# Head norm of mixer B's prompt on 32 partitions by 128 columns, and ScalarE's third key copy ahead of the prompt's exponential

## What is computed

```
a = jax.nn.softmax(jnp.where(mask, s, -jnp.inf), axis=-1)
attn = a[:, :, 0] - lam * a[:, :, 1]
o = jnp.einsum('bhqk,bkhe->bqhe', attn, v)
def diff_head_norm(o, g, lam_init):
    o = o * lax.rsqrt(jnp.mean(o * o, -1, keepdims=True) + RMS_EPS) * g
    return o * (1.0 - lam_init)
```

## Time and profile before

| | us |
|---|---|
| median of 3 runs | 1525.13 |
| lowest and highest | 1523.01, 1525.96 |
| the profiled execution's own time | 1522.43 |
| its span, first to last instruction | 1520.6 |
| attention stage within it | about 660 to 1010 |
| last head norm and start of the output projection | about 1010 to 1031 |

### The profile page before, as it was taken

One profiled execution on the slowest core, in us unless ns is written; L12 is line 12 of the kernel. 1 busy time (PEld: TensorE's weight loads), 2 busy tenths in 40 slices (PEclk: granted clock), 3 DMA queues, 4 the chain that ended last, 5 costly groups with the idle time before them and its releaser, 6 DMA issues.

```text
span 1520.6 us, 31196 instructions
## 1 busy us (share of the span) xinstructions
PE 1429.7 (94%) x12051; PEld 1247.0 (82%) x12051; DVE 943.1 (62%) x1823; ACT 610.3 (40%) x1160; POOL 286.8 (19%) x300
## 2 busy tenths in 40 slices
PE   4999999999999999989999988889899999999996
PEld 4788899999998788856666655559799999999995
DVE  2222473699845743645666666666799943899554
ACT  4322541344413422245555555552554422454323
POOL 1000330455200200010010000000066501555000
PEclk8999999999999999999999999999999999999998
DMA  9996222333223133368999998853133223333221
GB/s 313 386 365 225 56 85 84 103 100 89 73 83 115 51 106 109 122 233 281 340 332 338 341 321 273 312 187 88 29 91 95 85 77 97 100 91 96 65 70 63
DMA packets 217583, 245.98 MB, mean 162 GB/s; under 512 B 10655, under 2 KB 154649, under 8 KB 217442
## 3 DMA queue, kind: packets, MB, share of 16 engines
q1 hardware_dynamic: 217218, 243.63, 48.6%
q10 hardware_dynamic: 224, 0.39, 0.1%
HBM read 236.91 MB, written 7.08 MB: 160 GB/s over the span
## 4 chain that ended last, share of the span: by engine, by line
PE 68%; issue 14%; DVE 10%; ACT 5%; DMA 2%; SPq 1%; POOL 1%; ACTq 0%; DVEq 0%; POOLq 0%
PE ps L1103 39%; PE ps L316 8%; PE ps L2155 4%; PE ps L2167 3%; PE ps L2220 3%; DVE ring_lo L1095 2%; PE ps L2201 2%; PE ps L1528 1%; PE ps L2240 1%; PE ps L300 1%; DMA wada<-in_w_ada_dram 1%; PE ps L2254 1%; ACT PTd L2383 1%; DVE xT L340 1%; DVE f2lo L1361 1%
## 5 line engine op out<-in xcount | busy, mean ns | idle before, releaser
L1095 DVE TENSOR_TENSOR ring_lo<-ring_raw,ring_hi 128x512 fp32r<-128x512 f32 (+1 forms) x299 | 271.5, 942 | 48.7 <-ACT ring_hi L1081 40.4
L1081 ACT ACTIVATE ring_hi<-ring_raw 128x512 fp32r<-128x512 f32 (+1 forms) x334 | 188.7, 610 | 200.9 <-DMA ring_raw<-in_ffn_w_out_dram 175.9
L1103 PE MATMUL ps<-f2hi,ring_hi 128*128 128x288 f32 x704 | 208.7, 296 | 0.0
L1103 PE MATMUL ps<-f2lo,ring_hi 128*128 128x288 f32 x704 | 207.7, 295 | 0.0
L1103 PE MATMUL ps<-f2hi,ring_lo 128*128 128x288 f32 x704 | 207.0, 294 | 0.0
L1103 PE MATMUL ps<-hhi,ring_hi 128*128 128x288 f32 x572 | 169.8, 297 | 3.2 <-DVE tmp L1338 1.7
L1103 PE MATMUL ps<-hlo,ring_hi 128*128 128x288 f32 x572 | 168.4, 294 | 0.0
L2155 PEld LDWEIGHTS ps<-ident,k_ring 128*128 128x128 f32 x832 | 92.7, 143 | 58.2 <-issue 39.0
L1103 PEld LDWEIGHTS ps<-f2hi,ring_lo 128*128 128x128 f32 x704 | 132.6, 188 | 0.0
L1103 PEld LDWEIGHTS ps<-f2hi,ring_hi 128*128 128x128 f32 x704 | 131.9, 187 | 0.5 <-issue 0.5
L1103 PEld LDWEIGHTS ps<-f2lo,ring_hi 128*128 128x128 f32 x704 | 132.2, 188 | 0.0
(11 more groups left out here) (332 smaller groups left out, 3075.5 us busy)
## 6 DMA issues: line engine op xcount, KB each, us to landing
wada<-in_w_ada_dram SPq DMA_DIRECT2D x18, 2048.0 KB, 13.7
ring_raw<-in_ffn_w_in_dram SPq DMA_DIRECT2D x140, 256.0 KB, 3.1
k_ring<-in_cache_diff_k_dram SPq DMA_DIRECT2D x128, 256.0 KB, 4.4
v_ring<-in_cache_diff_v_dram SPq DMA_DIRECT2D x124, 256.0 KB, 4.6
ring_raw<-in_ffn_w_out_dram SPq DMA_DIRECT2D x64, 256.0 KB, 2.7
k_ring<-in_cache_win_k_dram SPq DMA_DIRECT2D x16, 768.0 KB, 5.3
v_ring<-in_cache_win_v_dram SPq DMA_DIRECT2D x16, 768.0 KB, 7.2
w<-in_w_qkv_dram SPq DMA_DIRECT2D x23, 512.0 KB, 3.7
```

The source lines that it names most:

```text
L1081: eng.activation(hi_of(g, i)[:, 0:n, :], raw_of(g, i)[:, 0:n, :], ACT.Copy).then_inc(sem("g_hi"), 1)
L1095: eng.tensor_tensor(lo_of(g, i)[:, 0:n, :], raw_of(g, i)[:, 0:n, :], hi_of(g, i)[:, 0:n, :].bitcast(F32), ALU.subtract).then_inc(sem("g_lo ...
L1103: m = nc.tensor.matmul(ps[:, bank, 0:TH], w, x, start=(first and n == 0), stop=(last and n == 2), skip_group_check=True)
```

## The change

Two things. First, the mean of a head's squares is taken with four products of 32 columns of `one_v` by 128 tokens each, which land side by side on four groups of 32 partitions of bank 7, 128 columns wide (`mean_head`). So square root and reciprocal run on 128 columns instead of 512: one reciprocal in place of four. Four further products with `sel` spread the result over all partitions and 512 columns of bank 7 (`spread_head`), at the end of quarter 6 in the loop, ahead of the last quarter's values behind it. The last multiplication reads bank 7 instead of `rms`, and the prompt's values of the next head wait for it (`r_rms`) instead of for the square root (`r_std`).

Second, ScalarE copies key group 2 ahead of the prompt's exponential, in every quarter.

```diff
+            def mean_head(squares_):
+                for j in range(PT_):
+                    mm = pe.matmul(ps[32 * j:32 * j + 32, 7, 0:P], one_v[:, 0:32], squares_[:, j * P:(j + 1) * P], start=True,
+                                   stop=True, tile_position=(0, 32 * j))
+                mm.then_inc(sem("r_mean"), 1)
+            def spread_head(inverse):
+                for j in range(PT_):
+                    mm = pe.matmul(ps[:, 7, j * P:(j + 1) * P], sel[:, j, :], inverse[:, 0:P], start=True, stop=True)
+                mm.then_inc(sem("r_mean"), 1)
...
                     if norm_head(b, i, run, 3):
                         pe.wait_ge(sem("r_sq"), b - 4)
-                        pe.matmul(ps[:, 7, :], one_v[:], rms, start=True, stop=True).then_inc(sem("r_mean"), 1)
+                        mean_head(rms)
+                    if norm_head(b, i, run, 6):
+                        pe.wait_ge(sem("r_rs"), b - 4)
+                        spread_head(rms)
...
                     if alive(b):
+                        evacuate(b, i, 2)
                         prompt_exp(b, i, mixer_of(b, run))
-                        evacuate(b, i, 2)
...
-                    for piece, at_quarter in enumerate(reciprocal_quarters(b)):
-                        if norm_head(b, i, run, at_quarter):
-                            cols = slice(piece * P, (piece + 1) * P)
-                            eng.wait_ge(sem("r_std"), b - 4)
-                            eng.reciprocal(rms[:, cols], rms[:, cols]).then_inc(sem("r_rs"), 1)
+                    if norm_head(b, i, run, 5):
+                        eng.wait_ge(sem("r_std"), b - 4)
+                        eng.reciprocal(rms[:, 0:P], rms[:, 0:P]).then_inc(sem("r_rs"), 1)
```

More of the change, by code:

```diff
@@ L2272, in prompt_values @@
                 if positive(b - 4):
-                    pe.wait_ge(sem("r_std"), b - 4)
+                    pe.wait_ge(sem("r_rms"), b - 4)
                 if positive(hd):
@@ L2338, in attend_tensor @@
             pe.wait_ge(sem("r_sq"), 4)
-            pe.matmul(ps[:, 7, :], one_v[:], rms_last, start=True, stop=True).then_inc(sem("r_mean"), 1)
+            mean_head(rms_last)
             turn_weights(LAST, 7, False)
             for i in range(4, 8):
+                if i == 7:
+                    pe.wait_ge(sem("r_rs"), 4)
+                    spread_head(rms_last)
                 values(LAST, i)
@@ L2412, in body @@
                     if norm_head(b, i, run, 4):
-                        eng.wait_ge(sem("r_mean"), b - 4)
-                        eng.activation(rms, ps[:, 7, :], ACT.Sqrt, bias=stat[:, 5:6], scale=1.0).then_inc(sem("r_std"), 1)
+                        eng.wait_ge(sem("r_mean"), 2 * b - 9)
+                        eng.activation(rms[:, 0:P], ps[:, 7, 0:P], ACT.Sqrt, bias=stat[:, 5:6], scale=1.0).then_inc(sem("r_std"), 1)
             for g in (1, 4):
@@ L2426, in attend_scalar @@
             copy_weights(LAST, 6, False, 1)
-            eng.wait_ge(sem("r_mean"), 4)
-            eng.activation(rms_last, ps[:, 7, :], ACT.Sqrt, bias=stat[:, 5:6], scale=1.0).then_inc(sem("r_std"), 1)
+            eng.wait_ge(sem("r_mean"), 7)
+            eng.activation(rms_last[:, 0:P], ps[:, 7, 0:P], ACT.Sqrt, bias=stat[:, 5:6], scale=1.0).then_inc(sem("r_std"), 1)
             copy_weights(LAST, 7, False)
@@ L2540, in body @@
                         eng.tensor_scalar(stat[:, 41:42], stat[:, 40:41], -1.0, None, ALU.mult).then_inc(sem("d_neg"), 1)
[L2541 to L2547 removed]
+                    if norm_head(b, i, run, 5):
+                        eng.wait_ge(sem("r_std"), b - 4)
+                        eng.reciprocal(rms[:, 0:P], rms[:, 0:P]).then_inc(sem("r_rs"), 1)
+                    if norm_head(b, i, run, 7):
+                        eng.wait_ge(sem("r_mean"), 2 * b - 8)
                         head = QT[:, ds(b - 1, 1), 0:NPR].rearrange("p a t -> p (a t)")
[L2549 removed]
+                        eng.scalar_tensor_tensor(out=head, in0=head, scalar=stat[:, 4:5], in1=ps[:, 7, :],
                                                  op0=ALU.mult, op1=ALU.mult).then_inc(sem("r_rms"), 1)
@@ L2571, in keep_second, with invert @@
                 eng.tensor_tensor(QT[:, 4:8, cols], part[:], turned_o[:, :, 0:NS], ALU.add).then_inc(sem("d_out"), 1)
-            def invert(piece):
+            def invert():
                 eng.wait_ge(sem("r_std"), 4)
-                own = rms_last[:, piece * P:(piece + 1) * P]
-                eng.reciprocal(own, own).then_inc(sem("r_rs"), 1)
+                eng.reciprocal(rms_last[:, 0:P], rms_last[:, 0:P]).then_inc(sem("r_rs"), 1)
             def lower(d):
@@ L2592, in attend_vector @@
             lower(1)
-            invert(3)
             split_lo(wo, 1, 1)
@@ L2596, in attend_vector @@
             lower(3)
-            eng.wait_ge(sem("r_rs"), 4 * NB - 16)
+            eng.wait_ge(sem("r_mean"), 8)
             head = QT[:, LAST, 0:NPR]
-            eng.scalar_tensor_tensor(out=head, in0=head, scalar=stat[:, 4:5], in1=rms_last,
+            eng.scalar_tensor_tensor(out=head, in0=head, scalar=stat[:, 4:5], in1=ps[:, 7, :],
                                      op0=ALU.mult, op1=ALU.mult).then_inc(sem("r_rms"), 1)
```

6 lines of the change are left out of this document (1 added, 5 removed).

## The result

| | before | after |
|---|---|---|
| median, us (6 runs each) | 1523.62 | 1510.46 |
| lowest and highest | 1520.32, 1525.96 | 1504.76, 1512.46 |
| the profiled execution's own time | 1522.43 | 1510.83 |
| its span | 1520.6 | 1509.0 |

The ratio of the times is 0.9909 (95% interval 0.9893 to 0.9925): the change saves 0.9%, about 13 us. The forecast was 1515.4 us with a range from 1510.5 to 1521.8.

The account below looks back on a forecast made before the run. TensorE, busy 94% of the span, was taken to bound the kernel, so only earlier starts count. 1.8 + 0.15 + 5.7 + 2.0 = 9.7 us off the 1525.13 median gave 1515.4 us, range 1510.5 to 1521.8.

Parts of the forecast that it names:

- rival B: Sequences 1 to 4: full DMA queues turn their gain into key waits; 8.2 us saved, 1516.9 us; chance 0.08.
- A: Whole kernel: only the norm counts, later exponentials eat the swap's gain; 5.0 us saved, 1520.1 us; chance 0.16.
- C: Attention quarters: exponentials delayed behind the copy make the kernel slower, 14 us lost against 9.7 won, 1529.9 us; chance 0.06.
- D: Whole kernel: the chain finds another wait in each quarter, saving under 3 us, 1524 us; chance 0.08.
- Quarter 7: Mixer A's last quarters (0.7 to 3.7): the swap starts the scores 0.46 us earlier each, 1.8 us in all.
- Sequence 4: Quarter 4.7: scores could start earlier but VectorE's normalization sets top; 0.15 us taken, between 0 and 0.73.
- Norm sequences: Sequences 5 to 7: 2.2 us each for 5 and 6, 1.25 for 7; together 5.7 us, between 3 and 7.5.
- the step on 5.5: Quarter 5.5: copy ahead of table load starts scores 1.4 us earlier, leaving 0.65 us at TensorE's last keys of 5.6.
- Behind the loop: Last head's tail: two reciprocals go, the spread comes ahead of the last values; 2.0 us, between 0.9 and 2.5.
- L2558 can still move by about its full 1 us: Behind the loop: last values end at about 1018.7, 1 us before the scaling's old start of 1019.78.
- Changes of the tiling mode: Behind the loop: mean and spread add two changes each; draining would cost 0.8 us, making the sum 8.9 us.
- The clock: At 1003 to 1009 us: the fall to 1.2 GHz may go (2.7 us) or come elsewhere (1.7 to 2.7); neither taken.

Follow-up runs that it names:

- e1: The kernel before with ScalarE's swap (key copy ahead of exponential) alone, in every quarter: 1518.52 us, ratio 0.9973.
- e2: The changed kernel with ScalarE's old order, so only the head norm is new: 1513.85 us, ratio 0.9937 against the kernel before.
- e3: The kernel before with ScalarE's swap in the last quarter (7) of each sequence only: 1516.66 us, ratio 0.9968.
- e12: The changed kernel with ScalarE's old order in quarter 5 of the three norm sequences only: 5.3 to 6.3 takes 44.04 us against 43.99.
- e4: The kernel before, unchanged, profiled once more: 1521.74 us.
- e14: The changed kernel with the second w_o load held until the last sequence's fifth values quarter: last prompt values to L300's last group 21.06 us against 21.43.
- e13: e8 with the second w_o load held until the fifth quarter of the last sequence's values: 1506.32 us, ratio 0.9894 against the kernel before.
- e8: The changed kernel with reciprocal in quarter 6, multiplication at quarter 7's start, last head's spread behind the last values: 1507.28 us, 0.9904 against the kernel before.
- e5: The changed kernel, unchanged, once more: 1510.01 us, ratio 0.9922 against the kernel before.
- e9: The changed kernel with reciprocal in quarter 6 and multiplication at quarter 7's start, spread left in place: 1506.31 us, 0.9895 against the kernel before.

## Why the prediction was right where it was, and where it wasn't

**Right.** What bounds the kernel, and that both parts gain, the norm more than the swap. The scores of quarter 7 no longer wait; sequences 1 to 4 with the DMA queues at 0.98 give their gain in full, so rival B (loads) falls. A and C fall by e1, e2 and e3, and D by the median. Of the signs that were named, those of the loop are there: no 1.2 us wait in 5.7, 0.85 at 6.0, the stretch 914 to 961 down from 46.7 to 44.0 (44.5 said). Those behind the loop are not: L300's third group came 1.15 us nearer and not 2. The multiplication from PSUM costs nothing (0.74 us against 0.75), narrow mean (0.42) and square root (0.37) cost what the rows of other operations had given, the spread 1.16 against 1.09. In 4.7 the scores start early and VectorE's normalization takes it back: from 4.7 to 5.3 after loses 0.43 us (20.68 against 20.25).

**What failed.** The gain of the loop was put 2.9 us too low and that behind it 0.85 too high, so that the sum came nearer to the time than its terms did. The steps one by one:

**Quarter 7: 0.67 each, not 0.46.** The step that failed is the size of a wait, taken from the bracket. The bracket is the idle time between the end of one record and the start of the next; but with nothing to wait for, TensorE's scores start 0.17 us before the end that the previous record shows (quarter 1.7 above). So a wait of TensorE is worth its bracket and about 0.2 us more: 4 x 0.2 = 0.8 us.

**Sequence 4: 0.90, not 0.15.** 0.66 at the scores of 4.7 (0.73 was the bound) and 0.24 in the quarters before it, where I had set nothing. 0.43 of this is given back by 5.3, as said; so 0.47 stay.

**Norm sequences: 2.7 each, not 2.2.** The 4.7 to 5.7 piece gives 1.77 as forecast only because it holds those 0.43 given back: from 5.3 it is 2.20, against 1.75. Here the step on 5.5 failed. It had the copy ahead of the table load leave 0.65 us at TensorE's last keys of 5.6. These keys ended 1.0 us earlier (899.77 against 902.01, less the 1.24 that after was ahead at 5.3). But e12, without the swap in 5.5, has their end 10.81 us behind the scores of 5.4, and after has it 10.82 behind. So the 1.0 is not the swap's. It is the narrow mean's and square root's: 0.68 at 5.4 and 0.33 more at 5.5, 1.0 in place of the 0.85 counted, and it passes whole. The forecast had no term for it in 5.6: it took the gain there from the swap, which VectorE cancels. The other 0.1 of the 0.45 was not followed. Sequence 7 keeps 2.2 at its scores and 1.9 at the prompt's values, where I had left 1.25. The wait there is for the multiplication, just past the bounds that were named (0 to 0.3):

```profile
997.52 2.39 PE L2273 MATMUL ps<-PTp,VH 128*128 128x512 f32 x8 [0.37 <-DVE QT L2560]
```

**Behind the loop: 1.15, not 2.0.** The step "L2558 can still move by about its full 1 us" failed. The scaling stands 11.18 us behind pv in e4 (1018.53) and 10.84 in after (1008.36): it moved by 0.34. The reciprocal that went behind it gave 0.8 more at L300's second and third group. The scaling waits for the last values, which end later than 1.06 us behind the spread: 0.43 us more go by inside the 32 records, and with the pause e14 takes away 0.37 of the piece (21.43 to 21.06). About 0.3 are the spread ahead of them (e14 against e13, which differ in the two moves as well). What the remaining 0.2 are is open.

**Changes of the tiling mode.** The forecast weighed a rule of the Trainium skill, TensorEngine Tiling (Array Packing), section Key Properties, by which changing the mode drains the engine, at 0.8 us of the tail. The weight loads of after show gaps of 0.17 to 0.20 us where the modes change:

```profile
1001.37 0.16 PEld L2279 LDWEIGHTS ps<-k_ring,one_v 128*32 128x32 f32 x8 [0.17 <-ACT k_ring L2435]
1002.78 0.15 PEld L2221 LDWEIGHTS ps<-V,PTd 64*32 64x32 f32 x8 [0.20 <-issue]
1005.67 0.97 PEld L2285 LDWEIGHTS ps<-k_ring,sel 128*128 128x128 f32 x8 [0.20 <-DVE k_ring L2585]
```

By that rule, the trace agrees in so far as gaps of this size stand there; the first and the third end on work of another engine, so that only the second shows one alone (e8 has L2285's 0.20 with no engine named). The matmuls hide it: L2285's begin at 1005.67 and the record ahead ends, by its row, at 1005.74.

**The clock.** I took neither the fall that may go nor one that may come. That put at nothing a term that the runs show. The fall at 1003 us belongs to one execution, as e4 shows, but every trace with the old norm has a fall in its last sequences and none with the new norm has one in the loop. The fall in the profile before cost 2.45 us, one of 3.4 us in the loop costs about 1.1.

**The sum and the range.** The pieces give 11.7 us where the forecast had 9.7: 0.8 more for quarter 7 of mixer A, 0.8 for sequence 4 and what follows to 5.7, 1.0 for sequences 6 and 7, 0.2 for the way to the prompt's values, and 0.85 less behind it. The other part of the miss of 4.9 us is the base: three more runs put the median before at 1523.62, 1.5 us below the 1525.13 from which I subtracted. The remaining 1.4 us have the size of one or two falls of the clock in the loop, the term put at nothing. The mean granted clock of whole executions, side by side with before's, leans the same way on three chips (e2 0.9835 against 0.981, e5 0.984 against 0.982, e9 0.983 against 0.981) and not on the fourth (e13, 0.983 for both); 0.002 of it is, by my estimate, 6 us less at the lower clock, nearly two falls of 3.4 us. The start of the stage gives no share in the traces, since the scores of 0.7 start at 700.9 and 701.0 us in before and e4, and at 702.1 and 702.2 in after and e5. That the clock is the whole of the 1.4 us is not shown. The range failed at its foot for the same reasons: upper ends of all terms gave 1509.9 and I drew 1510.5 in, with none of it for the base, though the three runs lay 3 us apart. (1509.9 counts the 0.15 of quarter 4.7 twice; the same ends give 1510.05.)

## What to carry to other kernels

A wait read off a bracket in front of TensorE can understate what its removal gives, here by 0.2 us: ask how the same pair of records stands where nobody waits, and take the distance between starts. Follow one gain at a time down to the next copy that everybody waits for, and when two gains meet at one place, ask of each alone what it leaves there; the one that a later engine cancels may hide the one that passes. Work that a quarter's bound engine must do belongs into its idle time of another quarter: moving two instructions of VectorE made a norm sequence 1.2 us shorter without any new code. And a fall of the clock that stands elsewhere in the next execution can still belong to the kernel: count the falls over several traces of each.

## What was not expected of the hardware

- The start of sequence 0 (0.0 to 0.7) takes 36.2 to 38.5 us in the three traces with ScalarE's old order and 32.2 to 37.3 in the thirteen with the new one there, e3's in quarter 7 alone, with a wait for a key load of 1.3 to 4.8 us and clock falls around it. This scatter alone is more than the swap gives, and whether the swap gains here can't be read from it:

```profile
684.19 1.09 PE L2155 MATMUL ps<-ident,k_ring 128*128 128x128 f32 x8 [1.34 <-DMA k_ring<-in_cache_diff_k_dram]
```

```profile
687.79 1.97 PE L2151 MATMUL ps<-ident,k_ring 128*128 128x128 f32 x8 [4.04 <-DMA k_ring<-in_cache_diff_k_dram]
```

The first row is of e3, the second of e2. All other pieces of the loop repeat to 0.2 us between kernels that are alike there, clock falls aside, which is why the effects of 0.3 us above could be read at all.
